# Moving two weights' splits, two column sums and one wait around the recurrent layer of a two-layer decoder kernel

## The reference, cut to what matters

```python
mod = (cs @ ada_w[layer] + ada_b[layer])[:, None, :]
sh_m, sc_m, g_m, sh_f, sc_f, g_f = jnp.split(mod, N_MOD, axis=-1)
u = modulate(h, sh_m, sc_m)
...
# mixer: chunks of 128 tokens in order, 4 heads; C is the carried state
num = (w_inter[..., None] * einsum('bhvd,bhtd->bhtv', C, qb) + einsum('bhts,bhsv->bhtv', s_qk, vb))
C_new = decay[..., None, None] * C + einsum('bhs,bhsv,bhsd->bhvd', w_state, vb, kb)
...
hs = hs * lax.rsqrt(jnp.mean(jnp.square(hs), axis=-1, keepdims=True) + RMS_EPS)
hs = hs * norm_w.astype(F32) * jax.nn.sigmoid(o.astype(F32))
```

## Time and profile before

| | us |
|---|---|
| median of 3 runs | 2362.44 (2361.22 to 2363.58) |
| profiled execution, own time | 2365.69 |
| its span (first to last instruction) | 2364.0 |
| TensorE busy | 2232.1 |
| VectorE busy | 1255.6 |
| ScalarE busy | 684.2 |
| GpSimd busy | 185.4 |

### The profile page before, as it was taken

How to read it: one execution, slowest core, us unless ns; L and a number is a source line. 1 busy time by engine, 2 the same in 40 slices (tenths; PEclk the granted TensorE clock), 3 DMA queues, 4 the chain that set the end, 5 groups by cost and what they waited for, 6 DMA issues and landing times. The chain is left out here.

```text
span 2364.0 us, 28136 instructions
## 1 busy us (share of the span) xinstructions
PE 2232.1 (94%) x10398; PEld 1831.0 (77%) x10398; DVE 1255.6 (53%) x2153; ACT 684.2 (29%) x1328; POOL 185.4 (8%) x206
## 2 busy tenths in 40 slices
PE   4999799999999999999998986889899999999997
PEld 2788688777888888888887864578788888888886
DVE  6333565567546446446576546656743443543447
ACT  2311344152202202203245227915311321221221
POOL 0000120110000000000020004513000000000003
PEclk9999899999999999999999988999999999999999
DMA  6344553103233233233221101101211211210211
GB/s 250 120 115 127 126 114 132 54 19 117 70 98 115 71 98 115 71 98 114 73 81 57 57 32 54 37 33 39 72 54 36 71 38 33 71 44 27 71 36 72
DMA packets 49696, 183.96 MB, mean 78 GB/s; under 512 B 6400, under 2 KB 6576, under 8 KB 49104
## 3 DMA queue, kind: packets, MB, share of 16 engines
q1 hardware_dynamic: 42768, 161.50, 21.6%
q0 software_dynamic: 6096, 21.16, 3.8%
q10 hardware_dynamic: 752, 0.22, 0.0%
HBM read 174.43 MB, written 8.42 MB: 77 GB/s over the span
## 5 line engine op out<-in xcount | busy, mean ns | idle before, releaser
L1522 PE MATMUL ps<-uhi,whi 128*128 128x512 f32 x1152 | 452.3, 393 | 15.8 <-DVE ulo L988 7.2
L1524 PE MATMUL ps<-uhi,wlo 128*128 128x512 f32 x1152 | 450.2, 391 | 0.0
L1523 PE MATMUL ps<-ulo,whi 128*128 128x512 f32 x1152 | 450.2, 391 | 0.0
L1522 PE MATMUL ps<-whi,hhi 128*128 128x512 f32 x1024 | 401.6, 392 | 5.6 <-DVE resid L1326 5.6
L1523 PE MATMUL ps<-wlo,hhi 128*128 128x512 f32 x1024 | 400.3, 391 | 0.0
L1524 PE MATMUL ps<-whi,hlo 128*128 128x512 f32 x1024 | 400.3, 391 | 0.0
L1326 DVE TENSOR_TENSOR resid<-ps,resid 128x512 f32<-128x512 f32 x256 | 176.6, 691 | 363.0 <-PE ps L1524 343.5
L793 ACT ACTIVATE h_whole<-ps 128x512 f32<-128x512 f32 x128 | 76.4, 597 | 833.6 <-PE ps L1524 833.6
L1522 PE MATMUL ps<-whi,uhi 128*128 128x512 f32 x704 | 284.4, 404 | 12.3 <-DVE wlo L957 8.8
L957 DVE TENSOR_TENSOR wlo<-stage,whi 128x1024 fp32r<-128x1024 f32 x180 | 220.8, 1230 | 122.7 <-ACT whi L616 122.5
L1524 PE MATMUL ps<-whi,ulo 128*128 128x512 f32 x704 | 276.9, 393 | 0.0
(11 more groups left out here) (221 smaller groups left out, 2109.0 us busy)
## 6 DMA issues: line engine op xcount, KB each, us to landing
stage<-in_stream SPq DMA_DIRECT2D x276, 512.0 KB, 3.6
aux<-in_early SPq DMA_DIRECT2D x2, 2048.0 KB, 10.3
early_place<-in_early SPq DMA_DIRECT2D x2, 2048.0 KB, 19.7
resid<-in_xt SPq DMA_DIRECT2D x8, 512.0 KB, 24.8
resid<-in_x POOLq DMA_DIRECT2D x8, 512.0 KB, 7.7
resid_dram<-resid POOLq DMA_DIRECT2D x8, 512.0 KB, 3.0
resid<-resid_dram POOLq DMA_DIRECT2D x8, 512.0 KB, 3.6
out<-resid SPq DMA_DIRECT2D x8, 512.0 KB, 2.6
```

Source lines behind the costliest of these rows:

```text
L1522: pe.matmul(dst, left_hi, right_hi, start=start, stop=False)
L1523: pe.matmul(dst, left_hi, right_lo, start=False, stop=False)
L1524: return pe.matmul(dst, left_lo, right_hi, start=False, stop=stop)
```

## The change

Four things move. On ACT, `splits(20, 21)` goes from ahead of chunk 0's squares to behind chunk 0's tanh. On DVE, `preps(20, 21)` (the low parts) goes from the end of chunk 0 to chunk 1, behind `update(1, 0)` and ahead of that chunk's first `ada` step. On PE, the sum of G_F0 in chunk 4 goes from ahead of gate blocks 0 and 1 to behind them. The sum of SH_KV goes from behind chunk 7 to behind token block 0 of the gate's second half, and DVE's `take_mod(SH_KV)` goes behind `preps(22, 23)` to match it; PE's wait for all head outputs is taken out.

```diff
@@ ScalarE @@
                 if c + 1 < T:
                     keys_by_token(c + 1)
-                if c == 0:
-                    splits(20, 21)
                 for h in range(H):
                     act.wait_ge(raw_ready, 2 * c + h // 2 + 1)
...
                 evac_o(0, c)
+                if c == 0:
+                    splits(20, 21)
             splits(22, 23)
@@ VectorE @@
                 update(c, 0)
+                if c == 1:
+                    preps(20, 21)
                 more = range(2 * (c % 4), 2 * (c % 4) + 2)
                 adas((G_F0, SH_KV)[c // 4], more[0:1] if c else more)
...
                 v.tensor_tensor(factor, mean, r, ALU.mult).then_inc(f_ready, 1)
-                if c == 0:
-                    preps(20, 21)
-                else:
+                if c:
                     adas((G_F0, SH_KV)[c // 4], more[1:2])
                 update(c, 3)
-            take_mod(SH_KV)
             apply_gate(0, T - 1)
...
+            take_mod(SH_KV)
             diagonal(G_M0)
@@ TensorE @@
                 numerators(c, 0)
+                by_token(FIRST["o0"] + c, W_O, c, part=(0, 1))
                 if c == 4:
                     pe.wait_ge(c_updated, H * c)
                     sum_vector(G_F0)
-                by_token(FIRST["o0"] + c, W_O, c, part=(0, 1))
                 if c == 0:
                     pe.wait_ge(sum_read, SC_F0 + 1)
...
                 state(c, 3)
-            pe.wait_ge(c_updated, H * (T - 1))
-            sum_vector(SH_KV)
-            pe.wait_ge(hs_ready, H * T)
             for t in range(T):
                 if t < T - 2:
                     by_token(o_group(1, t), W_O + 4, t)
                 elif t == T - 2:
                     last_two(o_group(1, t), W_O + 4)
+                if t == 0:
+                    pe.wait_ge(c_updated, H * (T - 1))
+                    sum_vector(SH_KV)
                 if t == 1:
                     build_row(FIRST["gm0"], 1)
```

## The result

The changed kernel takes 2369.24 us (median of 8 runs, 2367.66 to 2372.47), the kernel before 2361.83 in the same comparison (8 runs). The ratio is 1.0032, 95% interval 1.0021 to 1.0043: slower by 7.4 us, with an interval that begins just above the 0.2% that counts as no change. The profiled execution took 2369.40 us with a span of 2367.7.

What follows compares the result with a forecast made beforehand. TensorE, busy 94% of the span, bounds the kernel, so only idle time and clock can change. Terms +0.4 + 0.5 + 3.6 = +4.5 us give 2367.0; own range 2361.5 to 2370.1, stated range 2360.5 to 2370.5.

Steps and rivals of the forecast that it cites:

- Part 1: Splits of w20 and w21: chunk 0's 9.84 us stall becomes one of 10.3 in chunk 1; +0.4 us net.
- Part 2: Sum of G_F0 behind gate blocks in chunk 4: the state product must wait for DVE; +0.5 us.
- Part 3: Sum of SH_KV behind token block 0: exposed behind w23's products, with half clock; +3.6 us, at worst +4.9.
- full again 4.3 us later as above: Behind chunk 7: half clock at 363.5 ends after 4.3 us, the length read after chunk 0's stall.
- My upper end: Behind chunk 7: clock low throughout, 7 us from the restart, the sum taking 3.34 us; +4.9 us.
- The structural part: Behind token block 0: at full clock the sum, now in the open, delays token block 1 by 1.7 us.
- B: Rival, chunk 1: the fetch doesn't hold row 2's stage load back; +0.1 us, 2362.5; chance 0.17 together with unchanged-time rival.
- C: Rival, chunk 1: row 2 lands before DVE needs it, so the stall simply goes; -7.8 us, 2354.6; chance 0.10.
- D: Rival, chunk 1 and behind chunk 7: both at worst through transfers, clock low throughout; +8.0 us, 2370.4; chance 0.13.

Runs made afterwards that it cites:

- part1: The kernel before with the move of w20's and w21's splits alone; 2362.29 us, ratio 1.0000 to before.
- fetch_later: The changed kernel, but GpSimd fetches chunk 3's rows only once row 2 of G_F0 has been used; 2367.20 us, ratio 1.0024 to before.
- x_later: The changed kernel, but GpSimd issues the eight loads of x only once w23's low part is made; 2361.34 us, ratio 1.0001 to before.
- filler: The changed kernel with 12 and 21 unread matmuls in TensorE's waits for w22 and w23 in token block 0; 2365.63 us, ratio 1.0012 to before.
- part3: The kernel before with only SH_KV's sum behind token block 0 and no wait for all outputs; 2368.00 us, ratio 1.0029 to before.
- parts12: The kernel before with w20's and w21's splits moved and G_F0's sum behind gate blocks 0 and 1; 2363.02 us, ratio 1.0008 to before.
- early_row: The kernel before with SH_KV's last row used sooner, w22 split sooner and no wait for all outputs; 2354.04 us, ratio 0.9968 to before.

## Why the prediction was right, and where its size was off

**The forecast** was slower by 4.5 us at the edge of what counts as no change, 2367.0, with a range to 2370.5; measured are 7.4 and 2369.24. The sign and the places were right; one term was too small. The prediction gave slower a chance of 0.43 and no change 0.45, so that it is slower was no firm call, and the measured time lies near the upper end of the range.

**Part 1** was costed at +0.4 and is -0.2 in interval A, within the spread of A; part1 alone measures no change. Each step came out: no idling at 254.6, the next fetch at 260.74 (forecast 261.0), row 2's load 8.4 us to landing, its `ada` step at 271.88 (272.3), the state product at 274.97 (275.4) behind a stall of 9.91 (10.3). The run fetch_later shows the cause of the slow load by taking the fetch away: 3.6 us instead of 8.4.

**Turns between queues.** The Trainium skill says in "DMA: Bandwidth & Descriptors", "Queues, rings and completion order", that a transfer engine takes turns between queues packet by packet. Beside the fetch of decay rows the traces don't agree: q0 had 91.4% and q1 no row from 263 to 265 us, and q1 moved its first packet between 267 and 268 us, four microseconds behind the issue of row 2's load (263.4). In x_later w23's load, with nothing beside it, moved its first packet about a microsecond behind its issue. Beside the loads of x in before the two queues did share evenly from 357.6 to 360.2 us:

```profile
q0 software_dynamic: 155, 0.57, 54.4%
q1 hardware_dynamic: 132, 0.52, 48.6%
```

But there too the load came late to its turn. It was issued at 354.1, and from 354.5 to 357 us q0 had 95.4% and q1 no row. So in both places q1 got nothing for 3 to 4 us behind the issue. Beside the loads of x the trace then agrees with the rule. What holds the first packets back wasn't tried.

**Part 2** was costed at +0.5; interval B gives +0.4. That this sum can bring half clock behind it, for 1.7 us more as in filler and fetch_later, the prediction didn't have.

**Part 3** was costed at +3.6 with an upper end of 4.9, and is +7.0 in interval C. This is the term that was mis-sized. Its step "full again 4.3 us later as above" failed: w23's products started at 363.73 and half clock ended at some 374.7, 11 us later, so that most of token block 1 was slow too. My upper end took 7 us from the restart at 354.06, the longest that I had read, and there is longer. The structural part, the exposed sum, was right: 1.7 forecast, 2.0 in filler. Half clock is 5.0 and not 1.9. In part3's own profile it ended during the sum, and C is +3.65. That this is my very number is luck of the one execution, the lowest of eight: the median of that kernel is 6.5 above before. In fetch_later it lasted to about 374.3, 11 us from w23's products at 362.94, as in the changed kernel; why it ends so late in two profiles and early in part3's stays open. The forecast treated an event of varying length as one of known length. That w23 and not the sum is what matters was right: in the medians x_later takes the whole loss away.

**The rivals.** B (load not held back) falls with the 8.4 us; C (the stall simply goes) with the 9.91. D named the right size (+8.0) for half a reason: the clock did stay low, while the worse transfer did not come (w23's load took 7.1 us against 7.0).

## What to carry to other kernels

A wait is worth only the time until the next thing is late, so follow the buffer and not the instruction: moving a use of a shared buffer later moves the load behind it, and what that load then meets is the price. Work that stands ahead of a late arrival is free; the same work behind it is paid in full (2.0 us here), and with it the slow clock that the idling has brought (5.0). Where an engine waits for a load, look for the instruction whose use of the buffer lets the load be issued, and move that one sooner.

## What the runs showed of the hardware

- Half clock after idling is no fixed cost. After two idle stretches of 3.0 and 3.6 to 3.7 us, with 2.7 to 2.9 us of work between, full clock returned 3.3 us after the second restart in part3 (361.90) and 11 us after it in the changed kernel (363.73), where it had not come back between the two; the pause of 2.6 us in the first MLP brought it in one execution and not in another. The two cases are worth 3.4 us of C and 2.9 us in the MLP.
- Half clock also followed a stretch with hardly any idling: 16 matmuls of one column and 0.26 us of idling, in two of five profiles with this order (filler, fetch_later), at 1.7 us.
- Keeping TensorE busy with matmuls that nobody reads kept full clock through both waits (filler) and gave back 5.0 us of interval C; the medians are 3.6 apart.
- A stage load of 512 KB took 3.4 to 3.6 us in x_later, early_row and fetch_later with nothing beside it, and 7.0 to 7.2 beside the loads of x. Behind a fetch of rows the load of the stall took 8.2 to 8.6 us when issued 2.7 to 3.0 us behind it (before, the changed kernel, parts12, x_later) and 6.8 to 7.0 when issued 4.0 to 4.8 us behind it (part1, part3, filler, early_row): it landed 10.9 to 11.6 us behind the fetch either way.
